# The SSD stage's B turned by VectorE and DMA instead of TensorE, with a panel load, a rounding and the state matmuls moved behind

## What is computed

```python
xbc = silu(causal_depthwise_conv(xbc, ssm_conv_w, ssm_conv_b))     # 4 taps
xs, bm, cm = split(xbc)                   # x: 32 heads of 64; B, C: 4 groups of 128
# chunked scan, per chunk of tokens:
cb     = einsum("blgn,bsgn->blsg", ck, bk)                 # C . B
y_diag = einsum("blsg,blsgj,bsgjp->blgjp", cb, decay, xk)
y_off  = einsum("blgn,bgjpn,blgj->blgjp", ck, state, exp(acs))
new_state = state * exp(last) + einsum("bsgn,bsgj,bsgjp->bgjpn", bk, w_in, xk)
```

## Time and profile before

| | us |
|---|---|
| median of 3 runs | 1673.22 (1673.22 to 1673.37) |
| the profiled execution | 1672.8, its span 1671.1 |
| DVE busy | 917.4 (55%) |
| ACT busy | 702.8 (42%) |
| POOL busy | 799.5 (48%) |

### The profile page before, as it was taken

The page is one execution under the profiler, slowest core; times in us unless marked ns, Lnnn a source line. Parts: engine busy times, 40 slices in busy tenths (PEclk is TensorE's granted clock), DMA queues, the critical chain, the costliest instruction groups (busy, mean ns, idle before and its releaser), DMA issues.

```text
span 1671.1 us, 21613 instructions
## 1 busy us (share of the span) xinstructions
PE 1658.7 (99%) x7747; PEld 1350.2 (81%) x7747; DVE 917.4 (55%) x1436; ACT 702.8 (42%) x977; POOL 799.5 (48%) x607
## 2 busy tenths in 40 slices
PE   9999999999999999999999999999999999999998
PEld 7777778788888888878878788788888888888887
DVE  7434583563525267798998979867365511111113
ACT  5333364432323134456574645785324422222232
POOL 3443344464545456443434354445455444654453
PEclk9999999999999999999999999999999999999999
DMA  6656522364636242243333424222222222332233
GB/s 214 202 176 210 175 105 101 119 244 154 215 121 231 101 175 101 81 162 113 129 124 131 145 101 151 101 76 101 101 76 101 101 100 88 139 126 88 90 124 101
DMA packets 73052, 221.11 MB, mean 132 GB/s; under 512 B 6784, under 2 KB 43648, under 8 KB 54304
## 3 DMA queue, kind: packets, MB, share of 16 engines
q1 hardware_dynamic: 65888, 186.17, 32.8%
q10 hardware_dynamic: 7104, 34.15, 5.8%
HBM read 204.49 MB, written 15.79 MB: 132 GB/s over the span
## 4 chain that ended last, share of the span: by engine, by line
PE 94%; DVE 4%; POOL 1%; ACT 1%; DMA 0%; issue 0%; SPq 0%; DVEq 0%; POOLq 0%; ACTq 0%
PE gemm_bank L590 25%; PE gemm_bank L583 24%; PE gemm_bank L584 24%; PE gemm_bank L621 4%; PE gemm_bank L637 4%; PE gemm_bank L630 2%; PE gemm_bank L625 2%; DVE aux_bank L2267 1%; PE gemm_bank L889 1%; PE aux_bank L1064 1%; DVE sq L2308 1%; PE aux_bank L745 1%; PE aux_bank L1069 1%; PE aux_bank L1049 1%; POOL h L561 1%; PE aux_bank L719 1%
## 5 line engine op out<-in xcount | busy, mean ns | idle before, releaser
L533 POOL TENSOR_TENSOR w_lo<-w_raw,w_hi 128x512 fp32r<-128x512 f32 x580 | 775.5, 1370 | 850.9 <-ACT w_hi L1324 833.4
L583 PE MATMUL gemm_bank<-a_hi,w_hi 128*128 128x512 f32 x1008 | 399.9, 397 | 0.0
L584 PE MATMUL gemm_bank<-a_lo,w_hi 128*128 128x512 f32 x1008 | 392.8, 390 | 0.0
L1324 ACT ACTIVATE w_hi<-w_raw 128x2048 fp32r<-128x2048 f32 x145 | 276.6, 1908 | 183.0 <-PE gemm_bank L590 129.8
L583 PE MATMUL gemm_bank<-b_hi,w_hi 128*128 128x512 f32 x680 | 265.4, 390 | 0.0
L584 PE MATMUL gemm_bank<-b_lo,w_hi 128*128 128x512 f32 x680 | 264.6, 389 | 0.0
L590 PE MATMUL gemm_bank<-a_hi,w_lo 128*128 128x512 f32 x1024 | 256.9, 393 | 0.0
L583 PEld LDWEIGHTS gemm_bank<-a_hi,w_hi 128*128 128x128 f32 x1008 | 189.2, 188 | 48.8 <-issue 10.1
L590 PEld LDWEIGHTS gemm_bank<-a_hi,w_lo 128*128 128x128 f32 x1024 | 191.2, 188 | 44.0 <-issue 4.9
L584 PEld LDWEIGHTS gemm_bank<-a_lo,w_hi 128*128 128x128 f32 x1008 | 189.3, 188 | 40.9 <-issue 2.4
L2267 DVE SCALAR_TENSOR_TENSOR aux_bank<-scratch,gcol,aux_bank 128x511 f32<-128x511 f32 (+16 forms) x240 | 167.7, 733 | 12.4 <-ACT aux_bank L1568 9.4
(11 more groups left out here) (414 smaller groups left out, 2168.8 us busy)
## 6 DMA issues: line engine op xcount, KB each, us to landing
w_raw<-weights_dram SPq DMA_DIRECT2D x146, 1024.0 KB, 4.8
arena<-ada_dram ACTq DMA_DIRECT2D x32, 768.0 KB, 4.3
probs_turned_rows<-arena SPq DMA_DIRECT2D x16, 256.0 KB, 2.9
probs_turned_rows<-scratch SPq DMA_DIRECT2D x16, 256.0 KB, 3.1
arena<-probs_turned_rows SPq DMA_DIRECT2D x32, 128.0 KB, 4.4
scratch<-probs_turned_rows SPq DMA_DIRECT2D x32, 128.0 KB, 4.2
acc<-cum_rows ACTq DMA_DIRECT2D x8, 512.0 KB, 3.9
x_turned_rows<-scratch SPq DMA_DIRECT2D x16, 256.0 KB, 2.2
```

Source lines behind the costliest of these rows:

```text
L533: ins = pool.tensor_tensor(wlo[s][:, w], raw[s][:, w], whi[s][:, w].bitcast(F32), ALU.subtract)
L583: pe.matmul(gemm_bank[bank][:, :], whi[slot][:, w], hi[:, k, :], start=(n == 0), stop=False)
L584: pe.matmul(gemm_bank[bank][:, :], whi[slot][:, w], lo[:, k, :], start=False, stop=False)
L1324: act.activation(whi[panel % 2][:, :], raw[panel % 2][:, :], ACT.Copy).then_inc(w_hi_ready, 1)
```

## The change

- PE's four transposes of b_t go. DVE gets turn_b, the same 32x32 block transpose as for x, after conv4(5) and ahead of the taps behind it; it writes to the buffer that x tiles 0 and 2 used and waits until all x stores have landed.
- SP stores the turned b to DRAM, waits for the landing, and moves it back in four DMAs, behind the last move of x and ahead of the loads of panels 7 to 10.
- ACT copies the moved b to b_n (out of SBUF, in block order, instead of PSUM) after the copy of tile 11 instead of before it. grp_round(11) goes from there to behind the first two heads (k = 0).
- On PE g(11) follows g(10); cb's matmuls come next, then third(0), and only then states(0); each of the three states now stands a third later. Thirds 3 and 4 and all behind are as before.
- x_turned counts 5 and x_stored 80 a group instead of 4 and 64.

```diff
@@ -207,6 +207,8 @@
                       for head in range(2)]
         turned_x = [state[:, 0, :], state[:, 1, :]]
         x_raw = [state[:, 2, :], cb]
+        b_raw_n = state[:, 1, :]
+        b_dram = nc.dram_tensor("b_turned_rows", [P, QT, P], F32, kind="Internal").ap()
         x_dram = [nc.dram_tensor(f"x_turned_rows{n}", [P, QT, P], F32, kind="Internal").ap() for n in range(4)]
         cum_dram = nc.dram_tensor("cum_rows", [SSM_HEADS, S], F32, kind="Internal").ap()
         sq_sum = dist[:, :]
@@ -341,7 +343,7 @@
         x_stored = sem("x_stored")
         x_moved = [sem(f"x_moved{n}") for n in range(2)]
         xdt_ready = sem("xdt_ready")
-        bt_done = sem("bt_done")
+        b_moved = sem("b_moved")
         bn_ready = sem("bn_ready")
         cb_done = sem("cb_done")
         cbm_ready = sem("cbm_ready")
@@ -465,7 +467,7 @@
                 load(2 * i + 1, 1)
 
             def store_x(i, n):
-                sp.wait_ge(x_turned, 4 * i + n + 1)
+                sp.wait_ge(x_turned, 5 * i + n + 1)
                 sp.dma_start(x_dram[n], turned_x[n % 2].rearrange("q (g x) -> q g x", g=QT)).then_inc(x_stored, 16)
 
             def move_x(i, n):
@@ -478,14 +480,21 @@
                 for n in (3, 4, 5, 6):
                     load(P_GRP + 8 * i + n, (P_GRP + n) % 2)
                 store_x(i, 0), store_x(i, 1)
-                sp.wait_ge(x_stored, 64 * i + 32)
+                sp.wait_ge(x_stored, 80 * i + 32)
                 move_x(i, 0)
                 move_x(i, 1)
                 store_x(i, 2), store_x(i, 3)
-                sp.wait_ge(x_stored, 64 * i + 64)
+                sp.wait_ge(x_stored, 80 * i + 64)
                 for n in (2, 3):
                     sp.wait_ge(xdt_ready, 4 * i + n - 1)
                     move_x(i, n)
+                sp.wait_ge(x_turned, 5 * i + 5)
+                sp.dma_start(b_dram, turned_x[0].rearrange("q (g x) -> q g x", g=QT)).then_inc(x_stored, 16)
+                sp.wait_ge(x_stored, 80 * i + 80)
+                rows = b_dram.rearrange("(p k) g x -> k p g x", p=QT)
+                for g in range(QT):
+                    sp.dma_start(b_raw_n[32 * g:32 * g + 32, :].rearrange("k (p x) -> k p x", p=QT), rows[:, :, g, :]) \
+                        .then_inc(b_moved, 16)
                 for n in (7, 8, 9, 10):
                     load(P_GRP + 8 * i + n, (P_GRP + n) % 2)
 
@@ -1078,27 +1087,22 @@
                     g(0), g(1), g(2), g(3)
                 for j in range(4, 11):
                     g(j)
-
-                pe.wait_ge(silu_ready, 6 * i + 5)
+                g(11)
+                pe.wait_ge(silu_ready, 6 * i + 6)
                 if not first:
                     pe.wait_ge(yskip, 4 * i)
-                for c in range(QT):
-                    mm = pe.transpose(aux[2][:, c * P:(c + 1) * P], b_t[:, c * P:(c + 1) * P], ident[:, :])
-                mm.then_inc(bt_done, 1)
-                g(11)
-                pe.wait_ge(silu_ready, 6 * i + 6)
                 for c in range(QT):
                     mm = pe.matmul(aux[3][:, c * P:(c + 1) * P], b_t[:, c * P:(c + 1) * P], c_t[:, c * P:(c + 1) * P],
                                    start=True, stop=True)
                 mm.then_inc(cb_done, 1)
+                third(0)
                 pe.wait_ge(bn_ready, i + 1)
                 states(0)
-                third(0)
+                third(1)
                 pe.wait_ge(cbm_ready, i + 1)
                 states(1)
-                third(1)
+                third(2)
                 states(2)
-                third(2)
                 third(3)
                 third(4)
                 pe.wait_ge(st_ready, 3 * i + 3)
@@ -1594,7 +1598,7 @@
                     act.wait_ge(freed(j), free_value(T_GRP + j) + 4 * i)
                     if n < 4:
                         if n >= 2:
-                            act.wait_ge(x_turned, 4 * i + n - 1)
+                            act.wait_ge(x_turned, 5 * i + n - 1)
                             act.wait_ge(xcopy, 4 * i + n - 1)
                         act.activation(e_row[n % 2], sq[:, n % 2, :], ACT.Silu).then_inc(silu_ready, 1)
                         act.wait_ge(silu_ready, 6 * i + n + 1)
@@ -1614,18 +1618,18 @@
                 c4_end(5)
                 src = bank_of(10)
                 act.activation(chunk(g_conv, 2 * i), src, ACT.Copy).then_inc(freed(10), 1)
-                act.wait_ge(bt_done, i + 1)
-                act.activation(b_n, aux[2][:, :], ACT.Copy).then_inc(bn_ready, 1)
                 src = bank_of(11)
                 act.activation(chunk(g_conv, 2 * i + 1), src, ACT.Copy).then_inc(freed(11), 1)
-                grp_round(11)
+                act.wait_ge(b_moved, 64 * i + 64)
+                act.activation(b_n.rearrange("k (c p e) -> k c p e", c=QT, p=QT),
+                               b_raw_n.rearrange("k (p c e) -> k c p e", p=QT, c=QT), ACT.Copy).then_inc(bn_ready, 1)
 
                 def exp_row(hh):
                     k = hh // 2
                     act.wait_ge(row_loaded[k % 3], (32 * i + 16 * (k // 3) if k % 3 == 0 else 16 * i) + 16)
                     if hh < 2:
                         act.wait_ge(xcopy, 4 * i + 4)
-                        act.wait_ge(x_turned, 4 * i + 4)
+                        act.wait_ge(x_turned, 5 * i + 5)
                     elif hh == 2:
                         act.wait_ge(cb_done, i + 1)
                     elif hh == 3:
@@ -1662,6 +1666,8 @@
                     if k == 1:
                         act.wait_ge(y_done, 8 * i + 2)
                         load_rows(3)
+                    if k == 0:
+                        grp_round(11)
                     for q in ((0,), (), (1,), (2, 3))[k]:
                         z_copy(q)
                 for q in range(2):
@@ -2314,10 +2320,16 @@
                         else:
                             ins.then_inc(freed(j), 1)
 
+                def turn_b():
+                    dve.wait_ge(silu_ready, 6 * i + 5)
+                    dve.wait_ge(x_stored, 80 * i + 64)
+                    dve.transpose(turned_x[0].rearrange("q (g c e) -> q c g e", g=QT, c=QT),
+                                  b_t.rearrange("q (c g e) -> q c g e", c=QT, g=QT)).then_inc(x_turned, 1)
+
                 def turn_x(k):
                     dve.wait_ge(silu_ready, 6 * i + k + 1)
                     if k == 2:
-                        dve.wait_ge(x_stored, 64 * i + 32)
+                        dve.wait_ge(x_stored, 80 * i + 32)
                     dve.transpose(turned_x[k % 2].rearrange("q (g c e) -> q c g e", g=QT, c=QT),
                                   e_row[k % 2].rearrange("q (c g e) -> q c g e", c=QT, g=QT)).then_inc(x_turned, 1)
 
@@ -2380,6 +2392,8 @@
                         turn_x(0), turn_x(1)
                     elif n == 3:
                         turn_x(2)
+                    elif n == 5:
+                        turn_b()
                     taps((4, 4, 3, 3, 2, 2)[n] if first else (3, 3, 2, 2, 2, 2)[n])
                     if n >= 3:
                         x_times_dt(n - 3)
```

## The result

The changed kernel takes **1694.31 us** (median of 4 runs, 1693.01 to 1694.59) against 1673.3 (1673.22 to 1673.81) of the kernel before: ratio 1.0124, 95% interval 1.0112 to 1.0136. It is 21.0 us slower. Its profiled execution took 1694.08, with a span of 1692.4 us; lines of the kernel have moved by 2 to 14 (PE's here by 9, ACT's by 4, DVE's by 6 to 14).

What follows compares the result with a forecast made beforehand. PE, busy for 99% of the span, was taken to bound the kernel. Waits at outputs(0) of 3.5 + 3 x 3.1 = 12.8 us, added to the profiled 1672.8 plus 0.4 for the median, gave 1686.0 us, range 1677 to 1694.

Steps and rivals of the forecast that it cites:

- What bounds it: Whole kernel: PE, busy for 99% of the span, so a change gains only what it takes from PE.
- part 1: PE's transposes go: 4 x 0.48 = 1.9 us gained, plus 0.5 from group 0's wait for masked cb.
- Part 2: b's way through DVE and DRAM: b_n ready at about 841.5, 1.5 us before PE needs it in group 1.
- Part 3: turn_b's 0.64 us on DVE: costs 0 in groups 1 to 3 and 0.5 in group 0.
- Part 4: Panel 7's later load costs 0; its later rounding lets POOL's low parts start at 849.0 in group 1.
- Part 5: POOL's low parts and DVE's weigh take turns, delaying outputs(0) by 3.5 + 3 x 3.1 = 12.8 us.
- Rival C: Behind PE's waits at outputs(0): the turns plus a clock fallen to 1.2 GHz, 1692 up to 1698 us; chance 0.17.
- Rivals B and D: At weigh: DVE keeps the port (B, 1670.4 to 1674, chance 0.10); low parts are no obstacle (D, 1670.4, 0.03).

Runs made afterwards that it cites:

- e8_taps: Changed kernel, panel 7's load before x's moves, rounding right behind b_n's copy, two DVE taps later, states(1) and states(2) earlier on PE: 1671.65 us, ratio 0.9988.
- e3_early: Changed kernel with panel 7's load back ahead of b's store and its rounding back ahead of b_n's copy: 1682.52 us, ratio 1.0050.
- e1_fill: Changed kernel with 12 filler matmuls, results unused, in PE's wait ahead of outputs(0): 1686.47 us, ratio 1.0078.

## Why the prediction was wrong

The forecast was 1686.0 with a range of 1677 to 1694; the time is 1694.3, just above it. The direction and the mechanism were right, and one term was left out of the sum.

- **What bounds it, and part 1** (4 x 0.48 us gained on PE): right. Groups 1 to 3 of e8_taps keep 0.53 to 0.56 us each.
- **Part 2, b in time**: right, to a tenth. In group 1, less the 6.17 us by which it lies later: store at 834.50 (forecast 834.45), b_n's copy at 840.88 (840.89), no wait of PE. Group 0, with a wait of up to 0.3 us forecast, had none either.
- **Part 3, turn_b absorbed by POOL's turn**: right. x_times_dt(2) took 1.94 in place of 2.51 us and the taps behind it start at 843.67 - 6.17 = 837.50, where they started before.
- **Part 4**: the times were right (POOL at 855.39 - 6.17 = 849.2, forecast 849.0; in group 0 751.22, forecast 751.3). The cost of nothing for the load's new place was right too; e3_early shows the other side: with the load ahead of it b's way took 3.8 us longer.
- **Part 5, the turns**: right in size. outputs(0) of group 1 at 862.76 - 6.17 = 856.6 (forecast 856.45), of group 0 at 757.99 (758.05). The waits came to 12.7 us, the sum was 12.8. The single steps of group 1 held as well: less 6.17, next_state(2)'s line ends at 851.06 (forecast 850.85), weigh's four at 852.76, 854.31, 855.97 and 856.45 (852.55, 854.1, 855.8, 856.3).
- **Rival C, the clock**: here is the step that failed. The sum has no term for a fallen clock; full clock behind the waits was taken as the likelier case. I gave the fall 0.17 because PE's idle stretches of 3.6 to 4.1 us had no counterpart in the middle of the trace of before, and put 4 x 1.5 us on it "up to 1698". It came in every group of the profiled execution (mean granted clock 0.992 to 0.993 in all four executions, against 0.996 to 0.999 in those of the kernel before), and cost 2.70 + 1.62 + 2.60 + 1.63 = 8.55 us. 1686.0 + 8.55 = 1694.6, and with the clock kept up by e1_fill the time is 1686.47. Rows 10 told that the clock falls when PE is idle at the end; with no row that shows a 3.6 us gap that the clock survives, full clock should not have been the likelier case. Nor should the range have ended inside C's own values, 1692 to 1698. There was bad luck in it too: the one trace of before is the only one of thirteen without a fallen clock at 658 to 662 us, so that a mid-course fall could not be seen in it.
- **Rivals B and D** did not occur: DVE was held up first (line 2365, 1.79 us) and from then on they alternated.

The Trainium skill (TensorE: Matmul & The Clock Gate, Part 1) has a busy engine at 2.4 GHz and one that has idled at 1.2; the windows at 0.50 behind the waits agree, and so does e1_fill, in which PE was kept busy and the clock stayed at 1.00.

## What to carry to other kernels

An operation put off into another engine's idle time moves all that hangs on it: look up what the engines behind it (here POOL behind ACT's rounding) will run beside, and whether both read two SBUF operands. Each encounter costs the waiter up to one piece of the other's work, and a wait on the path often costs again, as the next encounter or as PE's clock. So price a PE idle stretch of 2.4 us or more at its length plus 1.3 to 2.7 us for the clock, as a likely case and not as a rival, and do not take one trace at full clock for proof that it stays full. Keep PE busy in it where it can't be removed, and after taking work from PE shorten what would end last next, or the gain turns into a wait.

## What the runs showed of the hardware

- Once a DVE operation with two SBUF inputs has waited for a POOL piece, they alternate piece by piece: 1.62 us for a 0.55 us operation beside 1.29 us pieces, 1.07 to 1.09 us beside half pieces.
- The clock fell behind 11 of 16 PE waits of 2.4 to 3.0 us and behind all four of 3.5 to 3.9 us; behind none of up to 1.8 us. What was lost each time was 1.3 to 2.7 us.
- It fell also, in twelve of thirteen profiled executions, during or just behind 32 matmuls of one or two columns, without a wait over 0.23 us.
- A store of 256 KB issued 0.8 us behind a load of 1 MB from the same queue took 5.9 us to the point where its landing had been seen and the next issue began, against 2.1 us alone.
